# One chip core, a pooling and mLSTM transformer: the third tile of the second FFN reordered, and ScalarE's copy of the first summed product moved ahead of the next tile's weight splits

## The reference, cut to what matters

```python
def _conv_ffn(h, w_in, conv_w, conv_b, w_out, grid):
    u, g = jnp.split(h @ w_in, 2, axis=-1)
    g = _dwconv_grid(g, conv_w, conv_b, grid)      # 3x3 taps on a 16 x 64 grid
    return (jax.nn.silu(g) * u) @ w_out
```

## Time and profile before

| | us |
|---|---|
| median of three runs | 2458.96 (2454.9 to 2459.98) |
| the profiled execution | 2454.94, its span 2453.0 |
| TensorE matmuls busy, of the span | 2349.1 (96%) |
| VectorE busy | 1671.3 (68%) |
| GpSimd busy | 894.6 (36%) |
| ScalarE busy | 815.2 (33%) |
| second FFN pass | about 1740 to 2437 |

### The profile page before, as it was taken

One profiled execution on the slowest core, in us unless ns is written; L12 is line 12 of the kernel. 1 busy time (PEld: TensorE's weight loads), 2 busy tenths in 40 slices (PEclk: granted clock), 3 DMA queues, 4 the chain that ended last, 5 costly groups with the idle time before them and its releaser, 6 DMA issues.

```text
span 2453.0 us, 35946 instructions
## 1 busy us (share of the span) xinstructions
PE 2349.1 (96%) x13630; PEld 1921.7 (78%) x13630; DVE 1671.3 (68%) x2156; ACT 815.2 (33%) x1187; POOL 894.6 (36%) x448
## 2 busy tenths in 40 slices
PE   7989999999999999999999998889979999999996
PEld 5557777787778778999889997767658888888884
DVE  4477888888888875553454306723757777889986
ACT  3642111111112125563443333333623333333333
POOL 0012122221212125663322005630576666666653
PEclk9999999999999999999999999989989999999998
DMA  8651212221122244653121238811211111111113
GB/s 345 232 198 78 86 44 84 86 86 64 65 86 86 82 175 160 219 180 113 55 75 59 71 108 218 230 52 69 69 44 57 55 51 51 51 60 69 68 43 137
DMA packets 106689, 255.10 MB, mean 104 GB/s; under 512 B 8928, under 2 KB 62816, under 8 KB 92128
## 3 DMA queue, kind: packets, MB, share of 16 engines
q1 hardware_dynamic: 89024, 228.56, 27.0%
q10 hardware_dynamic: 17568, 25.17, 2.8%
HBM read 223.68 MB, written 30.02 MB: 103 GB/s over the span
## 4 chain that ended last, share of the span: by engine, by line
PE 86%; DVE 5%; ACT 3%; DMA 2%; POOL 2%; issue 2%; SPq 0%; ACTq 0%; DVEq 0%; POOLq 0%
PE ps L737 18%; PE ps L739 17%; PE ps L738 17%; PE ps L1371 5%; PE ps L1373 5%; PE ps L1372 5%; PE ps L1123 2%; PE ps L1124 2%; PE ps L1125 2%; PE ps L839 1%; PE ps L1276 1%; PE ps L774 1%; PE ps L872 1%; PE ps L1014 1%; PE ps L790 1%
## 5 line engine op out<-in xcount | busy, mean ns | idle before, releaser
L3014 POOL TENSOR_TENSOR w_lo<-raw,w_hi 128x2048 fp32r<-128x2048 f32 x57 | 266.8, 4681 | 651.7 <-ACT w_hi L1645 291.3
L737 PE MATMUL ps<-hx_hi,w_hi 128*128 128x512 f32 x848 | 338.2, 399 | 2.5 <-ACT mix_out_c L1799 1.0
L739 PE MATMUL ps<-hx_lo,w_hi 128*128 128x512 f32 x848 | 331.3, 391 | 0.0
L738 PE MATMUL ps<-hx_hi,w_lo 128*128 128x512 f32 x848 | 331.2, 391 | 0.0
L2421 DVE TENSOR_TENSOR y_x<-y_x,ps 128x1024 f32<-128x1024 f32 x176 | 214.7, 1221 | 61.4 <-PE ps L739 56.6
L2403 DVE SCALAR_TENSOR_TENSOR acc<-ps,fcv,acc 128x945 f32<-128x945 f32 (+2 forms) x176 | 215.0, 1222 | 37.1 <-ACT acc L1689 16.0
L2926 DVE TENSOR_TENSOR y_x<-y_x,ps 128x512 f32<-128x512 f32 x304 | 206.9, 687 | 40.8 <-PE ps L739 40.8
L2873 DVE SCALAR_TENSOR_TENSOR acc<-ps,fcv,acc 128x945 f32<-128x945 f32 (+2 forms) x176 | 215.0, 1222 | 16.2 <-DVE acc L2873 2.3
L737 PEld LDWEIGHTS ps<-hx_hi,w_hi 128*128 128x128 f32 x848 | 159.8, 188 | 40.1 <-DVE hx_lo L2560 2.5
L739 PEld LDWEIGHTS ps<-hx_lo,w_hi 128*128 128x128 f32 x848 | 159.8, 188 | 34.0
L738 PEld LDWEIGHTS ps<-hx_hi,w_lo 128*128 128x128 f32 x848 | 160.0, 189 | 30.5
(11 more groups left out here) (414 smaller groups left out, 5616.9 us busy)
## 6 DMA issues: line engine op xcount, KB each, us to landing
raw<-in_ffn_w SPq DMA_DIRECT2D x44, 1024.0 KB, 6.6
modw<-in_modw SPq DMA_DIRECT2D x48, 512.0 KB, 7.0
raw<-in_ffn_w SPq DMA_DIRECT2D x44, 512.0 KB, 5.7
f_raw<-in_ffn_w SPq DMA_DIRECT2D x22, 1024.0 KB, 5.1
modw<-in_modw SPq DMA_DIRECT2D x21, 1024.0 KB, 4.8
raw<-in_mlstm_w SPq DMA_DIRECT2D x14, 1024.0 KB, 5.3
fw_raw<-in_ffn_w SPq DMA_DIRECT2D x22, 512.0 KB, 3.7
vch<-v_scr SPq DMA_DIRECT2D x18, 512.0 KB, 4.4
```

Source lines behind the costliest of these rows:

```text
L737: pe.matmul(out, whi, hhi, start=first, stop=False)
L738: pe.matmul(out, wlo, hhi, start=False, stop=False)
L739: return pe.matmul(out, whi, hlo, start=False, stop=last)
L3014: pool.tensor_tensor(w_lo[:, slot, 0:2048], raw[:, slot, 0:2048], w_hi[:, slot, 0:2048].bitcast(F32), ALU.subtract)\
```

## The change

- The order of tile 2 is redone. ScalarE splits u2's weights behind s3's instead of ahead of the t operands, and no part of tile 3 is split before tile 2 is finished. GpSimd makes u2's low part last, and s3's low part between the two halves of t3's. In the tile behind it (`fourth`, tile 3) `gated_low` and `out_low` come first.
- TensorE in tile 2 waits for the low parts of a t operand by halves, the first ahead of k = 0 and the second ahead of k = 2.
- SP loads fw_raw for tile 1 ahead of f_raw for tile 3.
- In tiles 3 to 20 ScalarE's copy of s1 stands ahead of the next tile's first weight split (g1) and of `out_high`; in the last tile it stands ahead of `out_high`.

```diff
@@ -116,7 +116,7 @@
 
 GATE_FIRST = ("g1", "g2", "s1", "s2", "s4", "s3", "u2")
 ORDER = ("g1", "s1", "s2", "s4", "s3", "g2", "u2")
-MADE_THIRD = ("s1", "g1", "g2", "u2", "s2", "s4", "s3")
+MADE_THIRD = ("s1", "g1", "g2", "s2", "s4", "s3", "u2")
 PLAIN = 2
 MOVING = {"g1": "x11", "g2": "x21", "s1": "t1", "s2": "t2", "s4": "x22", "s3": "t3", "u2": "t4"}
 BANK_A, BANK_B, BANK_C, BANK_G, BANK_Y = 2, 3, 4, 0, 5
@@ -705,11 +705,13 @@
             sp.wait_ge(sem("c_shifted"), SECOND["c_shifted"] + 8)
             sp.wait_ge(sem("pool_low"), SECOND["pool_low"] + 2)
             mod_half(0)
+            out_in(1)
+            halves_in(3)
             with sp.Fori(0, 6) as i:
                 for e in range(2):
-                    halves_in(i * 2 + (3 + e))
-                    out_in(i * 2 + (1 + e))
-            for j in range(13, FT - 1):
+                    halves_in(i * 2 + (4 + e))
+                    out_in(i * 2 + (2 + e))
+            for j in range(14, FT - 1):
                 if j + 2 < FT:
                     halves_in(j + 2)
                 out_in(j)
@@ -1361,12 +1363,14 @@
                         if h == 1:
                             first_half(8 * d + k)
 
-            def product(name, made, third=False):
+            def product(name, made, third=False, low=None):
 
                 pe.wait_ge(sem("lo_in"), made)
                 q, p = MOVING[name], slot_of(third, name)
                 out = ps[:, PRODUCT_BANK[name], :]
                 for k in range(KH):
+                    if low is not None and k % 2 == 0:
+                        pe.wait_ge(sem("pool_low"), low + k // 2 + 1)
                     ws = slice(P * k, P * k + P)
                     pe.matmul(out, p_hi[p][:, ws], x_hi[q][:, k, :], start=(k == 0 and name in ("g1", "g2", "s1")), stop=False, skip_group_check=True)
                     pe.matmul(out, p_lo[p][:, ws], x_hi[q][:, k, :], start=False, stop=False, skip_group_check=True)
@@ -1440,19 +1444,13 @@
                     pe.wait_ge(sem("mod1_done"), FT)
                     product("g2", made("g2"))
                 pe.wait_ge(sem("dve_moved"), j * 3 + (summed - 2))
-                if third:
-                    pe.wait_ge(sem("pool_low"), SECOND["pool_low"] + 12)
-                product("s1", made("s1"), third)
+                product("s1", made("s1"), third, SECOND["pool_low"] + 10 if third else None)
                 pe.wait_ge(sem("act_moved"), j * 4 + (moved + 1))
-                if third:
-                    pe.wait_ge(sem("pool_low"), SECOND["pool_low"] + 14)
-                product("s2", made("s2"), third)
+                product("s2", made("s2"), third, SECOND["pool_low"] + 12 if third else None)
                 pe.wait_ge(sem("act_moved"), j * 4 + (moved + 2))
                 product("s4", made("s4"), third)
                 pe.wait_ge(sem("act_moved"), j * 4 + (moved + 3))
-                if third:
-                    pe.wait_ge(sem("pool_low"), SECOND["pool_low"] + 16)
-                product("s3", made("s3"), third)
+                product("s3", made("s3"), third, SECOND["pool_low"] + 14 if third else None)
                 if not (third or last):
                     pe.wait_ge(sem("dve_moved"), j * 3 + summed)
                     product("g2", made("g2"))
@@ -2167,7 +2165,7 @@
             plain_moved(0, 1)
             for k in range(KH):
                 act.activation(x12_at[:, k, :], res_h[:, k, :], ACT.Identity, bias=shift(1, 1, "x", k)).then_inc(sem("c_shifted"), 1)
-            for name in ("g1", "g2", "u2"):
+            for name in ("g1", "g2"):
                 part_high(name, 2, True)
             for k in (0, 2):
                 act.wait_ge(sem("pool_low"), SECOND["pool_low"] + 1 + k // 2)
@@ -2223,20 +2221,27 @@
                 act.wait_ge(sem("dve_moved"), j * 3 + SECOND["dve_moved"])
                 act.activation(keep_a[:], ps[:, BANK_A, :], ACT.Copy).then_inc(sem("act_moved"), 1)
                 if third:
-                    part_high("s4", j, True)
-                elif not last:
+                    out_high(j - 1)
+                done("s1")
+                act.activation(fprod[:, par, TH:TX], ps[:, BANK_B, :], ACT.Copy).then_inc(sem("act_moved"), 1)
+                if not (third or last):
                     part_high("g1", j + 1)
                 if not third:
                     out_high(j - 1)
-                done("s1")
-                act.activation(fprod[:, par, TH:TX], ps[:, BANK_B, :], ACT.Copy).then_inc(sem("act_moved"), 1)
+                if third:
+                    part_high("s4", j, True)
                 done("s2")
                 act.wait_ge(sem("dve_moved"), j * 3 + (SECOND["dve_moved"] - 2))
                 act.activation(keep_b[:], ps[:, BANK_A, :], ACT.Copy).then_inc(sem("act_moved"), 1)
                 if third:
                     part_high("s3", j, True)
-                    part_high("g1", j + 1)
-                    out_high(j - 1)
+                    part_high("u2", j, True)
+                    silu(j - 1)
+                    gated_high(j - 1, 1 - par)
+                    finish(j, par, gate_first)
+                    for name in ("g1", "s1", "s2", "s4", "s3", "g2", "u2"):
+                        part_high(name, j + 1)
+                    return
                 if not last:
                     part_high("s1", j + 1)
                 silu(j - 1)
@@ -3136,15 +3141,20 @@
                 pool.wait_ge(sem("a_hi_ready"), j + (SECOND["a_hi_ready"] + 1))
                 pool.tensor_tensor(fa_lo[:, par, :], fprod[:, par, :], fa_hi[:].bitcast(F32), ALU.subtract).then_inc(sem("a_lo_ready"), 1)
 
-            def parts(j, par):
-
+            def parts(j, par, fourth=False):
+
+                if fourth:
+                    gated_low(j - 2, par)
+                    out_low(j - 2)
                 part_low("g1", j)
-                out_low(j - 2)
+                if not fourth:
+                    out_low(j - 2)
                 part_sum("s1", j)
                 part_sum("s2", j)
                 part_low("s1", j)
                 part_sum("s4", j)
-                gated_low(j - 2, par)
+                if not fourth:
+                    gated_low(j - 2, par)
                 part_low("s2", j)
                 part_low("s4", j)
                 part_sum("s3", j)
@@ -3184,20 +3194,21 @@
             for k in (0, 2):
                 pool.wait_ge(sem("pre_hi"), SECOND["pre_hi"] + 5 + k // 2)
                 moved(x_lo["t4"][:, k:k + 2, :], x21_at[:, k:k + 2], x_hi["t4"][:, k:k + 2, :].bitcast(F32))
-            part_low("u2", 2, True)
             for k in (0, 2):
                 moved(x_lo["t1"][:, k:k + 2, :], x_val["t1"][:, k:k + 2, :], x_hi["t1"][:, k:k + 2, :].bitcast(F32))
             part_sum("s4", 2, True)
             part_low("s2", 2, True)
             for k in (0, 2):
                 moved(x_lo["t2"][:, k:k + 2, :], x_val["t2"][:, k:k + 2, :], x_hi["t2"][:, k:k + 2, :].bitcast(F32))
+            part_sum("s3", 2, True)
             part_low("s4", 2, True)
-            part_sum("s3", 2, True)
-            part_low("s3", 2, True)
             for k in (0, 2):
                 pool.wait_ge(sem("pre_hi"), SECOND["pre_hi"] + 7 + k // 2)
                 moved(x_lo["t3"][:, k:k + 2, :], x_val["t3"][:, k:k + 2, :], x_hi["t3"][:, k:k + 2, :].bitcast(F32))
-            parts(3, 1)
+                if k == 0:
+                    part_low("s3", 2, True)
+            part_low("u2", 2, True)
+            parts(3, 1, True)
             with pool.Fori(0, FT // 2 - 2) as i:
                 parts(i * 2 + 4, 0)
                 parts(i * 2 + 5, 1)
```

## The result

| | median | lowest to highest | profiled execution | its span |
|---|---|---|---|---|
| before | 2458.96 us (7 runs) | 2454.9 to 2464.04 | 2454.94 us | 2453.0 us |
| after | 2466.35 us (7 runs) | 2463.32 to 2469.3 | 2467.4 us | 2465.3 us |

The ratio is 1.003, with a 95% interval of 1.002 to 1.0041: the changed kernel is 0.3% slower, 7.4 us by the medians. The prediction said 2455.0 us, between 2448 and 2462. Both are missed.

The account below looks back on a forecast made before the run. TensorE held 86% of the chain, but GpSimd's order set tile 2. Tiles 2 and 3 -10.7, eleven regular tiles +2.3, six tiles +4.4: -4.0 us on the 2458.96 median gave 2455.0 us, range 2448 to 2462.

Parts of the forecast that it names:

- step 5: Tile 2: VectorE's gate product comes in between GpSimd operations, delaying t3's second half about 1.0 us; u2 from about 1808.3.
- the 15.3 predicted: Tile 2: tile 1's output product starts at 1812.1 instead of 1827.38, so 15.3 us won.
- The 10.7 us predicted for both tiles: Tiles 2 and 3: tile 3 gives back part of the 15.3 us through its later f_raw load; 10.7 us left.
- the last term: Regular tiles: TensorE's output product starts 0.1 us behind gated_low's end, first pitch 0.08 longer; 0.2 us lost per tile.
- The term of the six tiles: Tiles 14 to 19, where VectorE also carries modulation work: 0.7 us lost each, 4.4 us in all, bounds 0.2 and 1.2.
- The rule weighed: VectorE operations with two SBUF inputs and GpSimd operations reading SBUF block each other; GpSimd next would give 2472 us.
- A: Rival: regular tiles have more cover and lose at most 0.1 us each; 2449.3 us, chance 0.35.
- C: Rival: second edit costs more than the first brings, at the gate product behind s1's low part; 2472 us, chance 0.15.

Follow-up runs that it names:

- second edit: ScalarE's copy of s1 ahead of the g1 split and out_high in tiles 3 to 21; alone on the kernel before: 2475.73 us, ratio 1.0071.
- the run with the small modulation steps: Changed kernel with VectorE's last modulation steps cut from 256 columns to 8 and to one SBUF input: 2462.38 us, ratio 1.0016.
- first edit: The new order of tile 2; alone, as the changed kernel with the copy of s1 put back: 2449.5 us, ratio 0.9958.
- the small sum's kernel: New order of tile 2 alone, plus an 8-column float32 GpSimd sum in tile 2: 2453.73 us, repeats 2453.89 and 2453.85.
- the execution with keep_b first: Kernel with the copy of s1 early in tile 3 alone, there with keep_b too ahead of the g1 split and out_high: 2453.67 us, ratio 0.9977.

## Why the prediction was wrong

**Tile 2: right in mechanism, 1.1 us short.** Set back by the 5.5 us of the start, s2 begins at 1794.3, as predicted, behind a wait of 1.72 us (1.8), and u2 at 1808.5 (1808.3). The clock stays. Tile 1's output product starts at 1813.2, and not at 1812.1. The step that failed is step 5: the gate product was to come in between two GpSimd operations, by the pattern of the earlier trace rows. It took 5.63 us. GpSimd got the 1.0 us back that this had been priced at, but ScalarE's gated_high then waited for the gate product, and gated_low started at 1813.92, behind 2.25 us of idle time. I had priced "in between or not" only in the regular tiles, and took it as settled in tile 2. Where the product did get in between (both executions with the second edit in tile 3 alone) tile 2 takes 44.94 and 44.93 us, 15.0 less than before: with the 0.5 us won ahead of it that is the 15.3 predicted.

**Tile 3: right, with one new loss.** s3 waits 0.97 us instead of 2.0, since TensorE comes 1.1 us later itself. The load, keep_b and the start of u2 come out within 0.4 us. Then the clock falls within u2, a cost that the prediction put at nothing:

```profile
1841.85 0.49 PE L1375 MATMUL ps<-t_hi,p_s_hi 128*128 128x512 f32 x1 [0.97 <-ACT keep_b L2235]
1849.39 0.49 PE L1375 MATMUL ps<-t_hi,p_u_hi 128*128 128x512 f32 x1 [1.81 <-DVE fprod L2907]
1853.71 0.51 PE L739 MATMUL ps<-fa_hi,fw_hi 128*128 128x512 f32 x1
```

u2's twelve matmuls take 4.32 us where twelve take 2.7; the granted clock is 0.89 from 1841 to 1856. The 10.7 us predicted for both tiles became 9.1.

**Ordinary regular tiles: 0.40 us and not 0.2.** The chain up to gated_low came out to a hundredth: SiLU at 9.55 (predicted 9.55), gate product to 12.59 (12.60), gated_low to 16.24 (16.25). What failed is the last term, "starts 0.1 behind such an end, with a first pitch 0.08 longer". TensorE starts 0.23 behind the end, at 16.46 to 16.50, and the first pitch is 0.10 longer. The ends of gated_low fit: 14.99 and 15.35 give 30.03 us, 16.24 gives 30.4, 16.39 gives 30.56. With a start 0.23 behind it, an end beyond 15.98 would delay a matmul wanted at 16.21 (an estimate from these rows). Mis-sized by 0.2 in eleven tiles, 2.1 us.

**Tiles 14 to 19: 1.97 us and not 0.7.** This is the step that decided the sign. I followed the chain GpSimd, gate product, ScalarE, GpSimd, and on VectorE looked at the second pair of modulation steps only. The first pair fell out. VectorE in tile 15 after the change, where g1 ends at 2203.90, and GpSimd beside it:

```profile
2214.52 1.98 DVE L2886 TENSOR_TENSOR fprod<-acc,fprod 128x1024 f32<-128x1024 f32 x1 [1.67 <-ACT acc L2204]
2216.42 0.67 DVE L2907 TENSOR_TENSOR fprod<-fprod,ps 128x512 f32<-128x512 f32 x1
2217.02 3.47 DVE L2390 SCALAR_TENSOR_TENSOR macc_x<-modh,c_pad,macc_x 128x256 f32<-128x256 f32 x2
2220.42 0.68 DVE L2915 TENSOR_TENSOR ps<-keep_a,ps 128x512 f32<-128x512 f32 x1
2221.01 2.35 DVE L2390 SCALAR_TENSOR_TENSOR macc_x<-modh,c_pad,macc_x 128x256 f32<-128x256 f32 x2
2223.28 10.58 DVE L2931 TENSOR_TENSOR y_x<-y_x,ps 128x512 f32<-128x512 f32 x16
```

```profile
2214.13 1.29 POOL L3131 TENSOR_TENSOR p_s_lo<-p_s_val,p_s_hi 128x512 fp32r<-128x512 f32 x1
2215.38 2.28 POOL L3121 TENSOR_TENSOR p_s_val<-f_raw,p_s_val 128x512 f32<-128x512 f32 x1
2217.75 2.46 POOL L3142 TENSOR_TENSOR fa_lo<-fprod,fa_hi 128x1024 fp32r<-128x1024 f32 x1
```

The gate product gets in behind s1's low part, as forecast. In turn s4's sum ends only at 2217.66 (1.0 later than alone), and the first modulation step, asked for at 2217.02, waits for it. Then gated_low starts at 2217.75, and the second step waits for its end at 2220.21. Two steps take 3.47 us instead of 1.06. gate_first_half comes 16.5 us behind g1 instead of 13.7, the second pair ends at 19.5 (predicted 18.1), and the first of the sixteen additions starts there. TensorE's fourth group then waits 1.22 us; I had 0.4 for the same wait. The term of the six tiles was put at 0.7 us each, 4.4 in all, and measures 11.8. With 0.7 each the regular tiles would have lost 8.5 us and not 16.1, and the kernel would have been about as fast as before.

**The rule weighed** said that two such operations block each other for the whole instruction, the first to issue winning (the Trainium skill, "SBUF — State Buffer", section "Who interferes with whom"). The trace agrees, in the gate product, s4's sum and both modulation steps. It left open who comes next of two that wait, and the runs show both answers in one kernel. The same section says that `tensor_scalar` can contend too, where its operands let it run in a two-port mode. The run with the small modulation steps agrees: two `tensor_scalar` steps of 8 columns took 3.16 us.

**The rivals.** A is out: no regular tile kept its cover. C's mechanism did not occur (the gate product ended at 12.59, s4's sum did not go first), but its sentence "the second edit costs more than the first brings" is what happened, 16.1 against 9.1 us, and past its own point of decision: the loss is 0.95 us per tile on average, where it said 0.9. I had joined it to a single mechanism with a single place, and so gave it too little. The bounds also were too narrow: 1.2 us at most for a tile of 14 to 19, though VectorE is busy 28.03 of 30.1 us there. The prediction used that figure against rival A and not for its own bound.

**The better version** is the first edit without the second: 2449.5 us (0.9958, 0.9946 to 0.997), or with it in tile 3 alone 2448.34 to 2449.39. That is 0.4% ahead of before, and 0.7% ahead of the changed kernel.

## What to carry to other kernels

When an edit shifts a chain on one engine by microseconds, write down every operation of the engine that shares SBUF with it in the new order of time, the small ones too. A step of 0.5 us that used to fall into a gap can be held for up to the 2.4 us of a neighbour, and what stands behind it with it. And an edit in a loop is priced times its trips: 17 tiles at 0.95 us outweigh a visible 9 us win, so the second edit needed a measurement of its own before it went with the first.

## What was not expected of the hardware

- A VectorE operation that asks while GpSimd works back to back took 2.1 us in four executions and 5.6 to 5.8 in seven, in the same place and at the same offset; one and the same kernel showed both.
- TensorE's start behind the end of a GpSimd operation: 0.23 us, then a first pitch of 0.33 against 0.23, with no wait in the profile's list. Small waits of this kind show only in the length of a tile.
- TensorE's clock fell from 2.4 to 1.2 GHz within a product behind shown waits of 0.97 and 1.81 us (tile 3 of after), and behind 1.83 us (the small sum's kernel), but stayed behind 1.72, 1.87 and 1.70 in tile 2 of after, and behind a lone wait of 3.31 in tile 3 of the kernel without the second edit (first row). In the execution with keep_b first, tile 2 has the same waits as after, each within 0.05 us, and there the clock fell within u2 (second row; granted clock 0.72 from 1810 to 1815):

```profile
1843.36 0.50 PE L1375 MATMUL ps<-x_hi,p_s_hi 128*128 128x512 f32 x1 [3.31 <-ACT fprod L2230]
...
1812.29 0.63 PE L1375 MATMUL ps<-t_hi,p_u_hi 128*128 128x512 f32 x1
```

Neither the length of the last wait nor the whole row of waits tells; what does stays open.
